# Prompt attention of a streaming encoder: two probability buffers per half, transposes two rounds behind the scores

## The reference

```python
qg = qb.reshape(B, blk, N_KV_HEADS, N_GROUPS, HEAD_DIM)
logits = jnp.einsum('btkgd,btskd->btkgs', qg, kg) * scale
logits = jnp.where(valid[:, :, None, None, :], logits, -jnp.inf)
p = jax.nn.softmax(logits, axis=-1)
o = jnp.einsum('btkgs,btskd->btkgd', p, vg)
```

## Time and profile before

| what | us |
|---|---|
| median of 3 runs | 4167.85 (4161.75 to 4168.66) |
| the profiled execution's own time | 4167.03 |
| its span, from the first to the last instruction | 4165.5 |
| the phase, from the first maxima to the last output product | 2367.8 to 2890.1 |

### The profile page before, as it was taken

How to read it: one execution, slowest core, us unless ns; L and a number is a source line. 1 busy time by engine, 2 the same in 40 slices (tenths; PEclk the granted TensorE clock), 3 DMA queues, 4 the chain that set the end, 5 groups by cost and what they waited for, 6 DMA issues and landing times. The chain is left out here.

```text
span 4165.5 us, 55709 instructions
## 1 busy us (share of the span) xinstructions
PE 3777.8 (91%) x19897; PEld 3306.9 (79%) x19897; DVE 2154.1 (52%) x3919; ACT 1086.2 (26%) x1841; POOL 220.5 (5%) x300
## 2 busy tenths in 40 slices
PE   6999999987999999988978689887888799999998
PEld 5988888876999999978964245553558699999997
DVE  5555555546444444455458767775323444444445
ACT  4322222323121111122123234342331312112111
POOL 2000000003000000011000000000000300000000
PEclk8888888878999999999976756666999999999999
DMA  2101011101111111111211100001421111111111
GB/s 87 37 32 37 32 37 37 37 11 33 41 41 46 41 46 36 46 39 54 83 67 41 51 11 11 1 1 59 155 118 41 33 41 41 46 41 46 41 41 58
DMA packets 58108, 187.20 MB, mean 45 GB/s; under 512 B 6984, under 2 KB 23376, under 8 KB 53520
## 3 DMA queue, kind: packets, MB, share of 16 engines
q1 hardware_dynamic: 53216, 165.23, 11.9%
q0 software_dynamic: 4656, 18.65, 1.4%
HBM read 164.28 MB, written 19.57 MB: 44 GB/s over the span
## 5 line engine op out<-in xcount | busy, mean ns | idle before, releaser
L206 PE MATMUL ff1lin<-ff1h_hi,ff1w_hi 128*128 128x384 f32 x1056 | 355.5, 337 | 25.7 <-POOL ff1h_lo L164 15.7
L206 PE MATMUL ff0lin<-ff0h_hi,ff0w_hi 128*128 128x384 f32 x1056 | 356.2, 337 | 22.8 <-POOL ff0h_lo L164 14.2
L207 PE MATMUL ff0lin<-ff0h_lo,ff0w_hi 128*128 128x384 f32 x1056 | 355.4, 337 | 0.0
L208 PE MATMUL ff0lin<-ff0h_hi,ff0w_lo 128*128 128x384 f32 x1056 | 355.1, 336 | 0.0
L208 PE MATMUL ff1lin<-ff1h_hi,ff1w_lo 128*128 128x384 f32 x1056 | 354.8, 336 | 0.0
L207 PE MATMUL ff1lin<-ff1h_lo,ff1w_hi 128*128 128x384 f32 x1056 | 354.8, 336 | 0.0
L206 PE MATMUL hg_lin<-hg_h_hi,hg_w_hi 128*128 128x384 f32 x768 | 269.2, 351 | 17.6 <-POOL hg_h_lo L164 15.7
L207 PE MATMUL hg_lin<-hg_h_lo,hg_w_hi 128*128 128x384 f32 x768 | 263.8, 343 | 0.0
L208 PE MATMUL hg_lin<-hg_h_hi,hg_w_lo 128*128 128x384 f32 x768 | 263.3, 343 | 0.0
L206 PEld LDWEIGHTS ff1lin<-ff1h_hi,ff1w_hi 128*128 128x128 f32 x1056 | 200.0, 189 | 28.1 <-POOL ff1h_lo L164 16.3
L206 PEld LDWEIGHTS ff0lin<-ff0h_hi,ff0w_hi 128*128 128x128 f32 x1056 | 200.3, 190 | 25.3 <-POOL ff0h_lo L164 14.8
(11 more groups left out here) (348 smaller groups left out, 8285.1 us busy)
## 6 DMA issues: line engine op xcount, KB each, us to landing
ff0raw<-in_weights SPq DMA_DIRECT2D x66, 512.0 KB, 3.5
ff1raw<-in_weights SPq DMA_DIRECT2D x66, 512.0 KB, 3.6
hg_raw<-in_weights SPq DMA_DIRECT2D x40, 512.0 KB, 3.5
as_keys<-in_cache_k SPq DMA_DIRECT2D x16, 1024.0 KB, 4.9
as_vals<-in_cache_v SPq DMA_DIRECT2D x8, 2048.0 KB, 9.3
pj_raw<-in_weights SPq DMA_DIRECT2D x18, 512.0 KB, 4.1
se_keys<-in_cache_ki SPq DMA_DIRECT2D x8, 1024.0 KB, 4.9
x<-in_x SPq DMA_DIRECT2D x3, 1536.0 KB, 7.1
```

Source lines behind the costliest of these rows:

```text
L206: pe.matmul(out, w_hi, x_hi, start=start, stop=False)
L207: pe.matmul(out, w_hi, x_lo, start=False, stop=False)
L208: return pe.matmul(out, w_lo, x_hi, start=False, stop=stop)
```

## The change

- `probs` and `neg_max` get a second buffer per half (by the parity of n). Maxima of round n wait for the transposes of round n-2, no longer of n-1.
- With `LAG = 2`, round n on PE is: scores of n half 0, transposes of n-2 half 0, scores of n half 1, transposes of n-2 half 1. The loops run three rounds longer.
- `values` follows the transposes of its fourth round, so it stands one round later than before. The product that spreads the reciprocals is taken out of it and stands one round later still (`spread_sums`). DVE's reciprocal stays where it was; its row form moves from the same round to two rounds later, and the final product from one round later to three (half 1).
- `q_hi` and `q_lo` hold one tile instead of two, and are made per round: ACT makes 128 columns in each round, six rounds ahead, POOL likewise (64 instructions each instead of 8). Every half's scores wait for `q_lo_set`, where only a tile's first ones did.

```diff
-    probs, probs_t = take("ap_probs", [P, 2, T_PROMPT]), take("ap_probs_t", [P, PT, 2, COLS])
-    q, q_hi, q_lo = take("ap_q", [P, 2, QB, P]), take("ap_q_hi", [P, 2, QB, P], F32R), take("ap_q_lo", [P, 2, QB, P], F32R)
+    probs, probs_t = take("ap_probs", [P, 2, 2, T_PROMPT]), take("ap_probs_t", [P, PT, 2, COLS])
+    q, q_hi, q_lo = take("ap_q", [P, 2, QB, P]), take("ap_q_hi", [P, QB, P], F32R), take("ap_q_lo", [P, QB, P], F32R)
...
-    part_max, neg_max = take("ap_part_max", [P, 2, 2]), take("ap_neg_max", [P, 2, 1])
+    part_max, neg_max = take("ap_part_max", [P, 2, 2]), take("ap_neg_max", [P, 2, 2, 1])
...
+    LAG, AHEAD = 2, QB - 2
...
-                    sp.wait_ge(q_lo_set, t - 1)
+                    sp.wait_ge(q_lo_set, QB * (t - 1))
...
-            for t in range(PT):
-                pool.wait_ge(q_hi_set, t + 1)
-                pool.tensor_tensor(q_lo[:, t % 2], q[:, t % 2], q_hi[:, t % 2].bitcast(F32), ALU.subtract).then_inc(q_lo_set, 1)
+            for n, (t, j) in enumerate(blocks):
+                pool.wait_ge(q_hi_set, n + 1)
+                pool.tensor_tensor(q_lo[:, j], q[:, t % 2, j], q_hi[:, j].bitcast(F32), ALU.subtract).then_inc(q_lo_set, 1)
...
-                if j == 0:
-                    pe.wait_ge(q_lo_set, t + 1)
+                pe.wait_ge(q_lo_set, n + 1)
                 if n:
                     pe.wait_ge(maxed, 2 * n + half - 1)
...
-                    i = pe.transpose(tr[c // 4][:, c % 4 * P:(c % 4 + 1) * P], probs[:, half, c * P:(c + 1) * P], const["ident"][:, :])
+                    i = pe.transpose(tr[c // 4][:, c % 4 * P:(c % 4 + 1) * P], probs[:, n % 2, half, c * P:(c + 1) * P],
+                                     const["ident"][:, :])
...
+            def spread_sums(u):
                 pe.wait_ge(inv_rows_set, u + 1)
                 pe.matmul(ib[:, :], sel_half[:, :], inv_rows[:, :, :].rearrange("r j t -> r (j t)"), start=True, stop=True)\
                     .then_inc(inv_done, 1)
 
-            for n in range(len(blocks) + 1):
+            for n in range(len(blocks) + LAG + 2):
+                m = n - LAG
                 for half in range(2):
-                    if n:
-                        turn(n - 1, half)
                     if n < len(blocks):
                         scores(n, half)
-                if n and n % GROUP == 0:
-                    values(n // GROUP - 1)
+                    if 0 <= m < len(blocks):
+                        turn(m, half)
+                if m > 0 and m % GROUP == 0:
+                    spread_sums(m // GROUP - 1)
+                if 0 <= m < len(blocks) and m % GROUP == GROUP - 1:
+                    values(m // GROUP)
...
-            def split_q(t):
+            def split_q(n):
+                t, j = blocks[n]
                 act.wait_ge(q_in[t % 2], 16 * (t // 2 + 1))
-                if t >= 2:
-                    act.wait_ge(qk_done, 2 * QB * (t - 1))
-                act.activation(q_hi[:, t % 2], q[:, t % 2], ACT.Copy).then_inc(q_hi_set, 1)
+                if t:
+                    act.wait_ge(qk_done, 2 * (n - QB + 1))
+                act.activation(q_hi[:, j], q[:, t % 2, j], ACT.Copy).then_inc(q_hi_set, 1)
...
-            split_q(0)
-            for n in range(len(blocks) + 1):
-                if n % QB == QB // 2 and n // QB + 1 < PT:
-                    split_q(n // QB + 1)
-                if n > 1 and (n - 1) % GROUP == 0:
-                    copy_inv((n - 1) // GROUP - 1)
+            for n in range(QB):
+                split_q(n)
+            for n in range(len(blocks) + LAG):
+                m = n - LAG
+                if m > GROUP and m % GROUP == 1:
+                    copy_inv(m // GROUP - 1)
                 for half in range(2):
-                    if n:
-                        t, j = blocks[n - 1]
-                        act.wait_ge(turned, 2 * (n - 1) + half + 1)
-                        act.wait_ge(pv_done, (n - 1) // GROUP)
+                    if m >= 0:
+                        t, j = blocks[m]
+                        act.wait_ge(turned, 2 * m + half + 1)
+                        act.wait_ge(pv_done, m // GROUP)
                         cols = slice(j % GROUP * P, (j % GROUP + 1) * P)
...
-                        act.activation(probs[:, half, 0:keys], probs[:, half, 0:keys], ACT.Exp, bias=neg_max[:, half],
+                        act.activation(probs[:, n % 2, half, 0:keys], probs[:, n % 2, half, 0:keys], ACT.Exp, bias=neg_max[:, n % 2, half],
                                        accum_out=total[:, u % 2, r:r + 1]).then_inc(exped, 1)
+                if QB <= n + AHEAD < len(blocks):
+                    split_q(n + AHEAD)
             copy_inv(len(groups) - 1)
...
-                if n:
-                    dve.wait_ge(turned, 2 * n + half - 1)
+                if n >= 2:
+                    dve.wait_ge(turned, 2 * (n - 2) + half + 1)
...
-            for n in range(len(blocks) + 1):
+            for n in range(len(blocks) + LAG + 2):
+                m = n - LAG
                 for half in range(2):
                     if n < len(blocks):
                         maxima(n, half)
-                    if n and n % GROUP == 0:
-                        (spread_inv if half else invert)(n // GROUP - 1)
-                    if n > 1 and (n - 1) % GROUP == 0 and half == 0:
-                        outputs((n - 1) // GROUP - 1)
+                    if half == 0 and n and n % GROUP == 0 and n <= len(blocks):
+                        invert(n // GROUP - 1)
+                    if half == 0 and m > 0 and m % GROUP == 0:
+                        spread_inv(m // GROUP - 1)
+                    if half == 1 and m > GROUP and m % GROUP == 1 and m < len(blocks):
+                        outputs(m // GROUP - 1)
                     if n < len(blocks):
                         u = 2 * n + half
                         search_on(steps_by[u - 1] if u else first_steps, steps_by[u])
```

More of the change, by code:

```diff
@@ L1684, in scores @@
                     out, keys = qk[half][c][:, 0:e - a], (rows, j // GROUP, slice(a, e))
-                    pe.matmul(out, q_hi[rows, t % 2, j, :], k_hi[keys], start=True, stop=False)
-                    pe.matmul(out, q_lo[rows, t % 2, j, :], k_hi[keys], start=False, stop=False)
-                    i = pe.matmul(out, q_hi[rows, t % 2, j, :], k_lo[keys], start=False, stop=True)
+                    pe.matmul(out, q_hi[rows, j, :], k_hi[keys], start=True, stop=False)
+                    pe.matmul(out, q_lo[rows, j, :], k_hi[keys], start=False, stop=False)
+                    i = pe.matmul(out, q_hi[rows, j, :], k_lo[keys], start=False, stop=True)
                 i.then_inc(qk_done, 1)
@@ L1801, in maxima @@
                 dve.wait_ge(qk_done, 2 * n + half + 1)
-                if n:
-                    dve.wait_ge(turned, 2 * n + half - 1)
+                if n >= 2:
+                    dve.wait_ge(turned, 2 * (n - 2) + half + 1)
                 parts = pieces((t + 1) * P)
                 for c, (a, e) in enumerate(parts):
-                    dve.tensor_tensor_reduce(out=probs[:, half, a:e], in0=qk[half][c][:, 0:e - a],
+                    dve.tensor_tensor_reduce(out=probs[:, n % 2, half, a:e], in0=qk[half][c][:, 0:e - a],
                                              in1=mask_p[:, mask_at(t) + a:mask_at(t) + e], scale=1.0, scalar=-3e38,
@@ L1812, in maxima @@
                     dve.drain()
-                dve.tensor_scalar(neg_max[:, half], part_max[:, half, 0:1], -1.0, None, ALU.mult).then_inc(maxed, 1)
+                dve.tensor_scalar(neg_max[:, n % 2, half], part_max[:, half, 0:1], -1.0, None, ALU.mult).then_inc(maxed, 1)
             def invert(u):
```

## The result

The changed kernel takes 4141.6 us (median of 4 runs, 4141.1 to 4147.5) against 4167.4 (4 runs, 4161.8 to 4168.7): ratio 0.9943, with a 95% interval of 0.9927 to 0.9959.

The account below looks back on a forecast made before the run. PE was taken to bound the kernel at half clock, DVE with its search at full clock. The terms -11 - 2.5 - 10 - 2 - 1 + 4.5 + 0.7 = -21.3 us took 4167.0 to 4145.7, forecast as 4146, range 4134 to 4156.

Parts of the forecast that it names:

- The exponential off the path (11): PE's next scores need the maxima alone, no longer the exponential: 11 us gained at half clock, bounds 0 and 17.
- the moved round of transposes (2.5): One more round of transposes leaves the loop to stand behind the last maxima: 2.5 us gained, bounds 0 and 3.9.
- The spreading product (10): Taken out of the values, where it delays PE's next work by 1.05 us in 11 blocks: 10 gained, bounds 0 and 11.6.
- POOL (+4.5): Narrow subtractions on POOL hold DVE's decisions: one hit in three at half of 0.5, some 4.5 us lost.
- the old wide division (2): ACT's and POOL's wide query instructions, which delayed PE and DVE, go: 2 us gained, bounds 0 and 13.
- The clock (1): The spreading product makes the stretch in which PE would fall back denser: 1 us gained.
- The end (+0.7): DVE's final product of the last group but one stands ahead of the last search: 0.7 us more at the end.
- The wait of the maxima for transposes: In the loop, maxima of n wait for transposes of n-2, behind the scores of n; no size was given.
- terms one and three: The exponential off PE's path (11 us gained, bounds 0 and 17) and the spreading product (10, bounds 0 and 11.6).
- the clock that stays up: Rival, 12%: PE holds its raised clock and DVE alone sets the loop, 442 instead of 494 us; time 4120.
- DVE take it back: Rival, 18%: PE's half-clock waits lie beside DVE's long search steps, so only 3 to 8 us gained; time 4161.

Follow-up runs that it names:

- a slower kernel (4154.5): Scores first, transposes one round behind, with each block of values cut by halves, the second half's products behind the next scores; 4154.5 us against 4168.4 before.
- one of 0.69 (4126.3): The changed kernel with LAG = 1: scores first, transposes one round behind instead of two; 4126.3 us against 4169.3 before, ratio 0.9897.

## Why the prediction came out as it did

The sign held and the time lies in the range. The bound (PE at half clock, DVE at full clock) is borne out, outside the blocks of values, by the kernel before: of DVE's 49.4 us in waits of under 3.5 us, 49.0 lie at half clock and 0.4 at full. By the table the loop's 32.1 us divide, in one order of steps, into spreading product 9.5, division per round 0, exponential and distance 6.2, scores ahead of transposes 16.4.

- *The exponential off the path (11) and the moved round of transposes (2.5).* The mechanism was right in part; its size was the step that failed: together 22.6 us instead of 13.5, outside their bounds of 0 and 20.9. The forecast took one cause, the exponential. The runs show two: with transposes ahead, two rounds of distance bring 6.2, of which up to 3.9 is the moved round, because ACT's copy of a half still stands behind an exponential. The other 16.4 come with the scores first. The text named that queue ("that copy is queued behind the exponential") and didn't ask whether distance removes it. The bound of 17 was also too low by its own rule: it took PE's waits before transposes at full clock as 22 x 1.29 = 28 us, but by the granted clock at each wait they are 19.7, in 13 waits, and 25.9 are left at half clock. With the change all of DVE's waits in the loop fell from 68.9 to 43.0 us at half clock and from 59.4 to 54.7 at full, and PE's idle time from 40.4 to 26.5 and from 19.9 to 17.7. So most of the gain in waits was at half clock, as the forecast had it, and there was more of it. DVE's waits of under 3.5 us alone fell from 49.4 to 35.2; with transposes ahead they are 54.2.
- *The spreading product (10).* Right where it was read, in the old order (9.5), but the terms were added as if independent: as the last step it is 4.6. It was also said to give nothing in tiles 1 and 2, where alone it gives 3.6.
- *POOL (+4.5) and the old wide division (2).* The duration was right (0.456 us for 0.48), the price was not: the narrow subtractions hold DVE for 2.0 us in all, the wide ones held it for 2.2, and both together, +2.5 in the forecast, measured as no difference. The wide division was not taken out alone.
- *The clock (1).* The granted clock rose to 0.65, within what was forecast. As told above, its part can't be kept apart from the waits.
- *The end (+0.7).* It is 1.0, and 0.35 more went ahead of the first maxima. 4.3 us came before the phase, which the change does not touch; the phase starts between 2334.0 and 2342.0 over all kernels here.
- *The wait of the maxima for transposes* was named ("maxima of n wait for the transposes of n-2, which stand behind the scores of n") and given no price. It costs 13 to 16 us, the largest thing left out. The sum could do without it only because the kernel before has one set of transposes in the same chain, ahead of the scores: the wait is no new loss, but it is a gain of scores first that was not taken.
- *The range (4134 to 4156).* Its lower end moves the terms together, its upper end only one at a time. With terms one and three at 0 and POOL at 12 together, the forecast's own sum gives about 4175. The upper end was too low.

Of the rivals, the clock that stays up did not come (0.65), nor did DVE take it back: that rival wanted a loop of 490 us with PE idle as before, and it is 462.0, with PE idle for 44.2 us instead of 60.3. The errors went against each other: the loop was 10 us shorter than forecast, what lies outside it 5 us longer, most of that ahead of the phase. That the forecast came within 4.4 us is in part luck.

## What to carry to other kernels

When an operation is moved further behind its producer, list what still joins the two: buffers written by the same round, and a shared PSUM bank whose release is queued behind the producer's work. Here distance two with two buffers put the transposes between scores and maxima, and distance one with the same buffers was 15 us faster. To see which waits can be gained, sort them by the granted clock at each: one row taken as typical for 22 waits gave 28 us where the trace has 19.7. Price the parts of a change also as the last one applied, not only as the first: one product was worth 9.5 us alone and 4.6 with the rest.

## What the runs showed of the hardware

- Matmuls of 64 output rows that alternate between rows 0 to 63 and 64 to 127 overlap: 8 took 1.94 us at full clock (0.24 each), 10 of one half 4.51 (0.45 each). In the fifth tile a block cut by halves took 5.85 + 4.51 us, one cut by keys 4.60 + 1.94; the clock rises within the first part of each.
- A small VectorE instruction on two float32 columns with one SBUF operand, started under a GpSimd subtraction, ends just behind it (up to 0.45 us instead of 0.17). Doubling the 56 GpSimd subtractions of 128 columns (0.456 us each) cost VectorE about 1 us in all.
- A granted clock of 0.77 in the loop went with a slower kernel (4154.5) than one of 0.69 (4126.3). The clock says how PE was used, not how fast the kernel is.
